# Two long-convolution mixers of a one-core kernel: the z projection as plain fp32 products, with the sums, the silus and the setup writes moved

## What is computed

```python
def conformer_conv_mixer(h, w_in, conv_w, conv_b, ln_g, ln_b, w_out):
    proj = h @ w_in                       # 1024 -> 3 x 2048
    val, glu_gate, z = jnp.split(proj, 3, axis=-1)
    u = val * jax.nn.sigmoid(glu_gate)
    u = causal_depthwise_conv(u, conv_w) + conv_b      # 31 taps
    u = jax.nn.silu(layer_norm(u, ln_g, ln_b))
    return (u * jax.nn.silu(z)) @ w_out   # 2048 -> 1024
```

## Time and profile before

| | |
|---|---|
| median of 3 runs | 1677.49 us (1676.03 to 1678.99) |
| profiled execution, own time | 1678.57 us |
| its span, first to last instruction | 1676.4 us |
| mean granted TensorE clock | 0.978 |
| first mixer, TensorE's first product to the last output half | 37.9 to 290 us |
| second mixer, the same | 836.3 to 1081 us |

### The profile page before, as it was taken

How to read it: one execution, slowest core, us unless ns; L and a number is a source line. 1 busy time by engine, 2 the same in 40 slices (tenths; PEclk the granted TensorE clock), 3 DMA queues, 4 the chain that set the end, 5 groups by cost and what they waited for, 6 DMA issues and landing times.

```text
span 1676.4 us, 28379 instructions
## 1 busy us (share of the span) xinstructions
PE 1591.5 (95%) x10947; PEld 1454.5 (87%) x10947; DVE 1056.3 (63%) x2144; ACT 862.7 (51%) x1552; POOL 556.0 (33%) x494
## 2 busy tenths in 40 slices
PE   4999879999999999999899988999999999999998
PEld 3888779988788999999888878988887777999998
DVE  3799975744565686666479998645035444775532
ACT  2577754543456454444357776543326555464442
POOL 0688842432222400000058895055511112200022
PEclk8999989999999999999999999998999999999999
DMA  4654335446553456665445434585652111657654
GB/s 129 141 142 137 126 114 176 165 154 132 119 123 126 152 166 189 181 194 179 125 126 145 132 127 134 168 175 136 179 170 79 51 58 57 195 167 201 172 158 128
DMA packets 341452, 240.10 MB, mean 143 GB/s; under 512 B 36925, under 2 KB 328475, under 8 KB 341320
## 3 DMA queue, kind: packets, MB, share of 16 engines
q1 hardware_dynamic: 329880, 231.33, 48.2%
q10 hardware_dynamic: 10992, 6.29, 1.8%
q0 software_dynamic: 448, 0.69, 0.5%
HBM read 236.55 MB, written 1.74 MB: 142 GB/s over the span
## 4 chain that ended last, share of the span: by engine, by line
PE 67%; DVE 18%; ACT 6%; issue 4%; POOL 3%; SPq 1%; DMA 1%; ACTq 0%; DVEq 0%; POOLq 0%
PE bank L682 7%; DVE bank L977 7%; PE bank L683 7%; PE bank L684 7%; PE bank L680 4%; PE bank L1091 4%; PE bank L731 3%; PE bank L1408 3%; PE bank L733 3%; PE bank L732 3%; DVE wlo L374 3%; PE bank L1409 3%; PE bank L1410 3%; ACT whi L365 2%; POOL scratch L920 1%
## 5 line engine op out<-in xcount | busy, mean ns | idle before, releaser
L374 POOL TENSOR_TENSOR wlo<-ring,whi 128x1024 fp32r<-128x1024 f32 (+3 forms) x132 | 296.1, 2246 | 710.3 <-ACT whi L365 710.2
L365 ACT CAST whi<-ring 128x1024 fp32r<-128x1024 f32 (+4 forms) x389 | 377.4, 990 | 259.5 <-PE bank L684 97.1
L374 DVE TENSOR_TENSOR wlo<-ring,whi 128x1024 fp32r<-128x1024 f32 (+4 forms) x257 | 342.4, 1340 | 247.8 <-ACT whi L365 246.2
L682 PE MATMUL bank<-xh,whi 128*128 128x256 f32 x1216 | 352.3, 290 | 13.1 <-POOL wlo L374 6.9
L683 PE MATMUL bank<-xl,whi 128*128 128x256 f32 x1216 | 347.9, 286 | 0.0
L684 PE MATMUL bank<-xh,wlo 128*128 128x256 f32 x1216 | 347.6, 286 | 0.0
L920 POOL TENSOR_TENSOR scratch<-scratch 128x256 f32<-128x256 f32 x288 | 211.2, 769 | 361.5 <-ACT scratch L865 357.8
L682 PEld LDWEIGHTS bank<-xh,whi 128*128 128x128 f32 x1216 | 237.4, 195 | 22.8 <-issue 19.4
L680 PE MATMUL bank<-sqb,ring 128*128 128x256 f32 x1024 | 230.7, 385 | 17.3 <-DVE xl L573 9.7
L680 PEld LDWEIGHTS bank<-sqb,ring 128*128 128x128 f32 x1024 | 197.2, 193 | 47.4 <-issue 10.5
L683 PEld LDWEIGHTS bank<-xl,whi 128*128 128x128 f32 x1216 | 237.7, 195 | 0.2
(11 more groups left out here) (284 smaller groups left out, 2930.6 us busy)
## 6 DMA issues: line engine op xcount, KB each, us to landing
ring<-in_a_w_in_dram SPq DMA_DIRECT2D x64, 512.0 KB, 5.2
ring<-in_b_w_in_dram SPq DMA_DIRECT2D x32, 1024.0 KB, 5.9
ring<-in_c_w_in_dram SPq DMA_DIRECT2D x64, 512.0 KB, 5.4
ring<-in_w_in_dram SPq DMA_DIRECT2D x26, 1024.0 KB, 5.3
ring<-in_w_ffn_in_dram SPq DMA_DIRECT2D x44, 512.0 KB, 5.1
ring<-in_a_w_in_dram SPq DMA_DIRECT2D x16, 1024.0 KB, 5.2
ring<-in_a_w_out_dram SPq DMA_DIRECT2D x16, 1024.0 KB, 5.0
ring<-in_w_ffn_out_dram SPq DMA_DIRECT2D x16, 704.0 KB, 4.6
```

The lines of the kernel that those rows point to most:

```text
L365: nc.scalar.copy(piece(whi, h)[:, :, 0:n], src).then_inc(hi_done, 1)
L374: engine.tensor_tensor(piece(wlo, h)[:, :, 0:n], src, piece(whi, h)[:, :, 0:n].bitcast(F32), ALU.subtract).then_inc(done, 1)
L682: nc.tensor.matmul(o, wh[:, k, :], xh[:, k, :], start=(k == 0), stop=False)
```

## The change

Five edits, in both long-convolution mixers:

1. All eight z units are plain. With that no projection of these mixers reads `xh` and `xl`, so the rms norm in front no longer makes them, and the first unit waits for `sqb` tile by tile. (The counters of the other norms are renumbered.)
2. z units 0 to 3 go to bank 2 and take no turn in banks 0 and 1; each waits for the silu of the z before it. z units 4 to 7 stay in banks 0 and 1. Shift's sum goes from bank 2 to bank 6.
3. TensorE's order at the end: the thirteenth sum and the eleventh square ahead of z unit 4, and all the remaining ones ahead of z units 5 to 7, regrouped.
4. ScalarE: the silu of z unit 3 stands among the taps of the last tile, that of unit 4 ahead of the square root, those of 5, 6 and 7 at tiles 6, 10 and 13 of the norm loop. The output units' splitting (`AHEAD_BESIDE`) starts at tile 8 with unit 0 and at tile 13 with unit 1.
5. The four DMAs of `write_skew` are issued by ScalarE behind tile 4's taps, not by GpSimd ahead of tile 2's.

```diff
@@ -426,7 +426,8 @@
             n["vg"], n["z"] = [], []
 
             def z_group(i):
-                n["z"].append((group((sz_done, j * 8 + i + 1)), unit_in(w, [(2 * E + i * 2 * P, 2 * P)], True)))
+                free = group((sz_done, j * 8 + i + 1)) if i >= 4 else None
+                n["z"].append((free, unit_in(w, [(2 * E + i * 2 * P, 2 * P)], plain=True)))
 
             for c in range(KE):
 
@@ -560,25 +561,13 @@
                 rms_square(act, ph, g)
             act.wait_ge(ss_done, ph + 1)
             nc.scalar.activation(std[:, 0:S], rms_bank[ph][:, 0:S], ACT.Sqrt, scale=1.0 / D, bias=eps).then_inc(std_done, 1)
-            for g in range(4):
-                act.wait_ge(xr_done, KD * ph + 2 * g + 2)
-                nc.scalar.copy(xh[:, 2 * g:2 * g + 2, :], sqb[:, 2 * g:2 * g + 2, :]).then_inc(xh_done, 1)
-
         def full_norm_dve(dve, ph):
             dve.wait_ge(std_done, ph + 1)
             nc.vector.reciprocal(rr[:, 0:S], std[:, 0:S]).then_inc(rr_done, 1)
             dve.wait_ge(rr_done, ph + 1)
-            def low(g):
-                dve.wait_ge(xh_done, 4 * ph + g + 1)
-                nc.vector.tensor_tensor(xl[:, 2 * g:2 * g + 2, :], sqb[:, 2 * g:2 * g + 2, :],
-                                        xh[:, 2 * g:2 * g + 2, :].bitcast(F32), ALU.subtract).then_inc(xn_done, 1)
-
             for k in range(KD):
                 nc.vector.scalar_tensor_tensor(sqb[:, k, :], xT[:, k, :], norm_g(GAIN[ph], k), rr[:, 0:S],
                                                ALU.mult, ALU.mult).then_inc(xr_done, 1)
-                if k % 2 == 1 and k >= 3:
-                    low(k // 2 - 1)
-            low(3)
 
         def rms_act(act, ph):
             raw_high(act, ph, 3)
@@ -598,7 +587,7 @@
             nc.scalar.copy(xh[:, 2 * g:2 * g + 2, :], sqb[:, 2 * g:2 * g + 2, :]).then_inc(xh_done, 1)
 
         def norm_low(dve, ph, g):
-            dve.wait_ge(xh_done, 4 * ph + g + 1)
+            dve.wait_ge(xh_done, 4 * RAW.index(ph) + g + 1)
             nc.vector.tensor_tensor(xl[:, 2 * g:2 * g + 2, :], sqb[:, 2 * g:2 * g + 2, :],
                                     xh[:, 2 * g:2 * g + 2, :].bitcast(F32), ALU.subtract).then_inc(xn_done, 1)
 
@@ -663,9 +652,9 @@
                 mm = nc.tensor.matmul(out, ll, rh, start=False, stop=(i == n - 1))
             return mm
 
-        def proj_T(pe, g, u, first=False, ph=0):
-
-            b = take_bank(pe, g)
+        def proj_T(pe, g, u, first=False, ph=0, at=None):
+
+            b = at if at is not None else take_bank(pe, g)
             for a, h in enumerate(hs(u)):
                 o = b[:, a * S:(a + 1) * S]
                 if is_split(h):
@@ -674,8 +663,10 @@
                 else:
                     landed(pe, u)
                 for k in range(KD):
-                    if first and a == 0:
-                        pe.wait_ge(xn_done, 4 * ph + k // 2 + 1)
+                    if first and a == 0 and is_split(h):
+                        pe.wait_ge(xn_done, 4 * RAW.index(ph) + k // 2 + 1)
+                    elif first and a == 0:
+                        pe.wait_ge(xr_done, KD * ph + k + 1)
                     if not is_split(h):
                         mm = nc.tensor.matmul(o, halves[h][1][:, k, :], sqb[:, k, :], start=(k == 0), stop=(k == KD - 1))
                         continue
@@ -818,15 +809,18 @@
             n_["y0"] = y0
 
 
-        Z_BESIDE = {1: 5, 5: 6, 11: 7}
+        Z_BESIDE = {6: 5, 10: 6, 13: 7}
+        AHEAD_BESIDE = {8: 6, 13: 7}
         OUT_BESIDE = {13: 0, 15: 1}
 
+        def z_bank(n, i):
+            return bank[2] if i < 4 else bank[n["z"][i][0] % 2]
+
         def conf_z(act, n, i):
 
-            g, u = n["z"][i]
-            act_ahead(act, u)
+            u = n["z"][i][1]
             group_done(act, u)
-            nc.scalar.activation(zb[:, 2 * i:2 * i + 2, :], bank[g % 2][:, :].rearrange("p (a t) -> p a t", t=S),
+            nc.scalar.activation(zb[:, 2 * i:2 * i + 2, :], z_bank(n, i)[:, :].rearrange("p (a t) -> p a t", t=S),
                                  ACT.Silu).then_inc(sz_done, 1)
 
         def conf_act(act, n):
@@ -853,8 +847,11 @@
             for c in range(KE):
                 act.wait_ge(u_done, j * KE + c + 1)
                 for i in range(TAPS_POOL):
-                    if i == TAPS_POOL // 3 and c + 1 < KE:
-                        sigmoid(c + 1)
+                    if i == TAPS_POOL // 3:
+                        if c + 1 < KE:
+                            sigmoid(c + 1)
+                        else:
+                            conf_z(act, n, 3)
                     if i == 2 * TAPS_POOL // 3 and c >= 3:
                         square(c - 3)
                     k = TAPS_DVE + i
@@ -864,17 +861,16 @@
                     bias = cols[:, ROWB + j * KE + c:ROWB + j * KE + c + 1] if i == 0 else 0.0
                     nc.scalar.activation(tmp[:, m % 4, :], src, ACT.Identity, scale=taps[:, j, k, c:c + 1],
                                          bias=bias).then_inc(tmp_done, 1)
+                if j == 0 and c == 4:
+                    write_skew(act)
                 if c == 2:
                     act.wait_ge(m0_done, j + 1)
-                    nc.scalar.activation(shift, bank[2][:, 0:S], ACT.Copy, scale=-1.0 / P).then_inc(shift_done, 1)
-            conf_z(act, n, 3)
-            square(KE - 3)
-            act_ahead(act, n["z"][4][1])
-            square(KE - 2)
-            square(KE - 1)
+                    nc.scalar.activation(shift, bank[6][:, 0:S], ACT.Copy, scale=-1.0 / P).then_inc(shift_done, 1)
+            for c in range(KE - 3, KE):
+                square(c)
+            conf_z(act, n, 4)
             act.wait_ge(var_done, j + 1)
             nc.scalar.activation(std[:, 0:S], std[:, 0:S], ACT.Sqrt, bias=eps).then_inc(lstd_done, 1)
-            conf_z(act, n, 4)
             for c in range(KE + 2):
                 if c >= 2:
                     y_high(act, n["y0"] + c - 2, y_hi[:, c - 2, :])
@@ -882,6 +878,8 @@
                     continue
                 if c in Z_BESIDE:
                     conf_z(act, n, Z_BESIDE[c])
+                if c in AHEAD_BESIDE:
+                    act_ahead(act, n["z"][AHEAD_BESIDE[c]][1])
                 if c in OUT_BESIDE:
                     act_ahead(act, n["out"][OUT_BESIDE[c]][2])
                 act.wait_ge(dn_done, j * KE + c + 1)
@@ -890,18 +888,16 @@
                 nc.scalar.activation(yb[:, c, :], yb[:, c, :], ACT.Silu, scale=lg, bias=lb).then_inc(act_done, 1)
             out_act(act, n)
 
-        def write_skew(pool):
-
-            pool.wait_ge(tab_copied, 4)
+        def write_skew(act):
+
+            act.wait_ge(tab_copied, 4)
             for v, (h0, nh) in enumerate(((0, 16), (16, 4), (20, 4), (24, 4))):
                 src = tabs[0:nh, v, :].unsqueeze(1).to_broadcast((nh, COPIES, TABLE))
-                pool.dma_start(skew[h0:h0 + nh, :, :], src).then_inc(skew_written, 16)
+                act.dma_start(skew[h0:h0 + nh, :, :], src).then_inc(skew_written, 16)
 
         def conf_pool(pool, n):
             j = n["j"]
             for c in range(KE):
-                if j == 0 and c == 2:
-                    write_skew(pool)
                 first = (j * KE + c) * TAPS_POOL
                 for i in range(2, TAPS_POOL):
                     if i == TAPS_POOL // 2 and c + 1 < KE:
@@ -921,10 +917,9 @@
                         .then_inc(tap_done, 3 if i == 3 else 1)
                 pool.wait_ge(tap_done, first + TAPS_POOL)
                 nc.gpsimd.tensor_tensor(accp[:, c % 2, 0, :], accp[:, c % 2, 0, :], accp[:, c % 2, 1, :], ALU.add).then_inc(pool_sum, 1)
-            lo_pool_to(pool, ahead(n["z"][4][1]))
             for c in range(KE):
-                if c in Z_BESIDE:
-                    lo_pool_to(pool, ahead(n["z"][Z_BESIDE[c]][1]))
+                if c in AHEAD_BESIDE:
+                    lo_pool_to(pool, ahead(n["z"][AHEAD_BESIDE[c]][1]))
                 if c in OUT_BESIDE:
                     lo_pool_to(pool, ahead(n["out"][OUT_BESIDE[c]][2]))
                 pool.wait_ge(act_done, j * KE + c + 1)
@@ -989,7 +984,6 @@
                     dve.wait_ge(raw_done, 3 * j + 3)
                     nc.vector.tensor_tensor(yb[:, 2, :], yb[:, 2, :], shift, ALU.add).then_inc(conv_done, 1)
             dve.wait_ge(conv_done, j * KE + KE)
-            dve_ahead(dve, n["z"][4][1])
             dve.wait_ge(mean_done, j + 1)
             dve.wait_ge(sqm_done, j * KE + KE)
             chain(dve, nc.vector.tensor_scalar(rr[:, 0:S], bank[7][:, 0:S], -1.0 / E, None, ALU.mult))
@@ -1005,8 +999,8 @@
             dve.wait_ge(lstd_done, j + 1)
             chain(dve, nc.vector.reciprocal(rstd, std[:, 0:S]))
             for c in range(KE + 3):
-                if c in Z_BESIDE:
-                    dve_ahead(dve, n["z"][Z_BESIDE[c]][1])
+                if c in AHEAD_BESIDE:
+                    dve_ahead(dve, n["z"][AHEAD_BESIDE[c]][1])
                 if c in OUT_BESIDE:
```

(23 more changed lines are left out.)

## The result

| | before | after |
|---|---|---|
| median (range) of 4 runs each | 1678.24 us (1676.03 to 1679.32) | 1635.17 us (1633.72 to 1643.84) |
| profiled execution, own time; span | 1678.57; 1676.4 us | 1643.84; 1642.0 us |
| mean granted TensorE clock | 0.978 | 0.988 |
| first mixer, first product to marker | 252.05 us | 232.66 us |
| second mixer | 244.62 us | 231.97 us |

The ratio of the times is 0.9757 (95% interval 0.9738 to 0.9776): 43 us faster at the medians, where 35 had been forecast. The forecast of 1642 was right in sign.

What follows compares the result with a forecast made beforehand. TensorE, busy 95% of the span, was taken as the bound, losing 30.8 and 23.3 us of the mixers to waits and half clock. Gains of 23.3 and 15.8, less 2 a mixer, gave 35 us: 1642, range 1636 to 1656.

Steps and rivals of the forecast that it cites:

- z unsplit: All 16 z units: TensorE pays 6.91 instead of 5.74 us each, +9.4 a mixer; casts and subtractions fall off other engines.
- The start: First unit of each mixer: TensorE waits for the first gain alone and starts 1.9 us earlier.
- the bounds: Clock at each mixer's start: 1.0 us lost if its rise stays put, 2.1 won if the clock stays up.
- Banks: Convolution, z 0 to 3 in bank 2: val/gate units never wait for a silu; no gain a period, TensorE loses its waits.
- Skew writes: DMA issues moved to ScalarE behind tile 4: about 2.6 us, covered by its waits, or 2.6 once without cover.
- Last sums ahead: End of the convolution, last sums ahead of three z units: statistics at 198.5, 12.3 us earlier.
- The norm loop: Normalised tiles at 1.20 us each undisturbed; splits at tiles 8, 13 and 15 ready about when TensorE asks.
- The rival that it still binds: Norm loop: late output splits keep TensorE waiting, 7.2 us a mixer lost, 1653 us; chance 0.22.
- a sign of being wrong: Output products: TensorE waiting for `wlo` at out 1 or out 2, half clock behind it, would show the forecast wrong.
- the 4.7 reckoned: Output unit 1 if the norm loop binds: it comes at 229.3 instead of 224.6, 4.7 us lost, plus 2.5 by half clock.
- the 2 us kept: Allowance of 2 us a mixer for tight places: last sums wait 1.0 for the last square, out 1 up to 1.0.
- The sum: Both mixers: ends move 23.3 and 15.8 us, 39.1 together; 35 after the allowance, arriving whole at the end.

Runs made afterwards that it cites:

- third execution: The changed kernel, unedited, timed a third time: median 1637.14 us, ratio 0.9754 to the kernel before.
- unsplit and silus only: Kernel before with z and start unsplit, silus of z 3 to 7 and remaining splits in new places, shift's sum in bank 2: 1642.69 us, ratio 0.9781.
- banks undone: Changed kernel with z units 0 to 3 taking their turn in banks 0 and 1 again: 1637.83 us, ratio 0.9765 to the kernel before.
- unsplit alone: Kernel before with the z units and the norm at the start unsplit, nothing else changed: 1644.57 us, ratio 0.981.
- the repetition: The changed kernel, unedited, timed again: median 1634.75 us, ratio 0.9753 to the kernel before.

## Why the prediction was right, and where it wasn't

*z unsplit.* Right, and the main thing. TensorE has unit 12 until 155.99 (155.4 forecast), the convolution ends at 197.43 (196.7), statistics at 199.19 (198.5), first normalised tile 204.37 (203.7), silu of z 5 at 210.18 (209.6). Each is 0.6 to 0.7 late, which is about what the start lost by the clock. TensorE's period of four tiles in the changed kernel is 38.0 (110.23 to 148.22), as forecast, without a wait in it.

*The start.* The first product came 1.86 us earlier (1.9 forecast). The clock's rise was assumed to move with it; it moved by about 0.7 us (42.5 to 41.8), and the first 128 products took 30.6 us where they had 30.1, so 0.5 was lost, between the bounds. In the second mixer it went the other way: the half clock was shorter than before, and the same products took 29.4 us where they had 30.2. In the third execution the half clock at the first start ended at 39, and in "unsplit and silus only" it never came:

```profile
34.00:38.00 4.00, 3.53 (x16) 3.14 (x17) 3.10 (x8) 0.00 (x0) 0.00 (x0) 1.00 0.00 0
```

The same instructions met the clock at another point in each execution. The Trainium skill (TensorE: Matmul & The Clock Gate, Part 1: The HAM clock gate) has the gate count without regard to where a kernel's matmuls begin; the trace agrees, by these three starts.

*Banks.* Wrong in its reasons: bank 2 was to rid the val/gate units of their wait for a silu, 1.7 us. It went with the splits alone, and banks undone brought back 0.31, for VectorE's product.

*Skew writes.* The mis-sized term. 2.6 us on ScalarE were taken from GpSimd's row; it was 8.0 (0.68 for the first and 7.32 for three). The cover, ScalarE's waiting for the next unit, wasn't enough: VectorE waited 1.87 us for a sigmoid at 102.00. TensorE didn't; by the periods, VectorE has 1.7 us in each to catch up. With z 0 to 3 split the same issues are followed by TensorE's wait of 5.37. And they bought nothing: VectorE's wait of 2.85 for shift went with GpSimd's split, as "unsplit alone" shows, so this part of the change put 1.87 where nothing would have been.

*Last sums ahead.* The statistics did come 11.6 us earlier, 12.3 forecast, but by the splits that no longer stand in front of them: in "unsplit alone", with the old order, they stand at 200.03. With only the order undone TensorE waits 0.7 instead of 0.3 and the time is the same. Forecast as a step of its own, it isn't one.

*The norm loop.* The rival that it still binds (1653) fell in the first mixer, where the only wait, 0.76 us, is at the second half of out 3. In the second it showed in small: the 1.60 us at 1003.10 is a wait for GpSimd's `wlo` at the first half of out 1 (two halves of 8 tiles lie between 995.40 and 1000.98), the very place that the prediction named as a sign of being wrong. It is a third of the 4.7 reckoned, without half clock behind it, and with the 0.28 at the last sums it stays inside the 2 us kept. It repeats to 0.1 us in every run that has the silus and splits in their new places. With the silus alone back in their old places the mixers are 8 us longer. The second mixer's pair was dearer as forecast: VectorE's subtraction 2.54 us at 1001.49, 1.23 at 213.49.

*The sum.* 39.1 less 2 + 2 kept for tight places. The second marker came 35.7 us earlier, so 3.4 of the 4 went. The tight places took 1.0 and 1.9; the first start lost 0.5 by the clock, and the second took 0.7 less than the 30.1 reckoned for it, by luck; the remaining 0.7 are small gaps that nothing here places. The sum is in work and waits and has no term for the clock outside the starts; it lands because the waits and half clock of the kernel before were taken together, as what lies between the measured length and the work. The profiled execution took 1643.84 where 1678.57 - 35 = 1643.6; that this is so near is chance, as the repetitions show. The step that failed is the next: "after both mixers the stages follow TensorE's end, so it arrives whole", and from the profiled execution to the median by the 1.1 us that lay between them before. The profiled execution of the changed kernel is 8.7 us above its median (it is the slowest of its set in each of the three runs of this kernel, so the profiles show the slower side), 5.4 of which is seen in the stages behind the mixers (596.8 against 591.4 in the repetition). Of the 5 to 8 us that the medians of the three gained beyond the forecast's 35, up to 4 are these stages in two of three executions; the rest is in executions without a trace and stays open. A range whose low end was set by the mixers' waits alone had no term for it.

## What to carry to other kernels

Splitting fp32 work into cheaper products pays only where the engines that make the halves have time: here each unit saved TensorE 1.2 us, 18.7 in all, and undoing that alone won 33 us of waits, half clock and late statistics. Where two engines lie close in a stage, here 36.3 and 38.0 us a period, price every edit on both, since taking from one is worth at most the distance to the other, and count what a wait costs again in clock. And a DMA issue is priced on the engine that will make it, not on the one that did.

## What was unexpected of the hardware

- Issuing the same four DMAs took 8.0 us on ScalarE's queue (0.68 for the first, beside a tap, and 7.32 for three) and 2.56 on GpSimd's; ScalarE's next activation began 7.39 us after the last one had ended.
- After gaps of about 3 us (3.04 ahead of the first product, 2.80 at 977.98) TensorE ran at half clock for some us, but for one start of one execution; six products into a bank about to be overwritten kept it at 1.00 in all four starts that had them, and the mixers were 1.6 to 2.9 us shorter.
- Stages that the change doesn't touch took 590 to 597 us from execution to execution, with waits at the same two places of 0.7 to 3.3 and 0.2 to 2.5 us.
